# The leads of four layers re-ordered: rounding ahead, squares by pairs, two additions on GpSimd instead of four, angles during the first load

## The reference

```python
def rms_norm(x, g):
    xf = x.astype(jnp.float32)
    y = xf * lax.rsqrt(jnp.mean(xf * xf, axis=-1, keepdims=True) + RMS_EPS)
    return (y * g.astype(jnp.float32)).astype(x.dtype)

for l in range(DEPTH):                       # first block
    xn = rms_norm(h, norm_mix[l])
    proj = xn @ w_in[l]
    ...                                      # attention with top-k keys, short conv, RWKV-7 scan
    h = h + mixed @ w_out[l]
    h = h + conv_glu_ffn(rms_norm(h, norm_ffn[l]), ffn_up[l], ffn_conv[l], ffn_down[l])
h = rms_norm(h, norm_final)
for layer in range(DEPTH):                   # second block
    u = rms_norm_2(h, norm_w[layer], RMS_EPS) @ w_in[layer]
    ...                                      # dilated and differential attention, gates
    h = h + merged @ w_out[layer]
return rms_norm_2(h, final_norm_w, RMS_EPS)
```

## Time and profile before

| | before |
|---|---|
| median of 3 executions | 1776.34 us (1774.9 to 1778.92) |
| profiled execution, its own time | 1774.47 us |
| its span, first to last instruction | 1772.6 us |
| busy: PE, DVE, ACT, POOL | 96%, 64%, 52%, 11% of the span |
| chain that ended last | PE 75%, DVE 14%, ACT 6%, POOL 2% |
| mean granted TensorE clock | 0.98 of full speed |

### The profile page before, as it was taken

How to read it: one execution, slowest core, us unless ns; L and a number is a source line. 1 busy time by engine, 2 the same in 40 slices (tenths; PEclk the granted TensorE clock), 3 DMA queues, 4 the chain that set the end, 5 groups by cost and what they waited for, 6 DMA issues and landing times.

```text
span 1772.6 us, 30818 instructions
## 1 busy us (share of the span) xinstructions
PE 1708.3 (96%) x13020; PEld 1548.0 (87%) x13020; DVE 1138.3 (64%) x1601; ACT 930.3 (52%) x1369; POOL 195.2 (11%) x214
## 2 busy tenths in 40 slices
PE   6999999899998999999999999999999989999998
PEld 5988999899997988998899998888788878887887
DVE  6867455576666966446676666656766546567654
ACT  5473424454445583424454455665674446656742
POOL 1453400100001544300100000000000010000000
PEclk8999999899999999999899999999999989999998
DMA  5433433345544433432455545434345444343451
GB/s 206 172 135 99 151 128 120 135 174 185 176 167 159 165 120 102 156 121 95 167 186 179 191 165 190 145 141 166 119 146 196 158 167 152 133 166 119 158 195 51
DMA packets 48057, 268.34 MB, mean 151 GB/s; under 512 B 13552, under 2 KB 14448, under 8 KB 16176
## 3 DMA queue, kind: packets, MB, share of 16 engines
q1 hardware_dynamic: 38448, 264.80, 42.0%
q10 hardware_dynamic: 8704, 0.53, 0.3%
q0 software_dynamic: 768, 1.05, 0.2%
HBM read 264.52 MB, written 1.84 MB: 150 GB/s over the span
## 4 chain that ended last, share of the span: by engine, by line
PE 75%; DVE 14%; ACT 6%; POOL 2%; issue 2%; DMA 1%; SPq 0%; DVEq 0%; POOLq 0%; ACTq 0%
PE bank L1328 13%; PE bank L1329 13%; PE bank L1330 13%; PE bank L2413 8%; PE bank L2415 8%; PE bank L2414 8%; DVE w_low L866 4%; ACT arena L2046 1%; ACT arena L613 1%; ACT w_high L550 1%; PE bank L2484 1%; DVE small L2271 1%; PE bank L1555 1%; PE bank L2443 1%; DVE arena L2267 1%
## 5 line engine op out<-in xcount | busy, mean ns | idle before, releaser
L866 DVE TENSOR_TENSOR w_low<-slab,w_high 128x2048 fp32r<-128x2048 f32 x250 | 581.6, 2330 | 248.3 <-ACT w_high L550 247.4
L1328 PE MATMUL bank<-act_high,w_high 128*128 128x256 f32 x2304 | 663.6, 288 | 8.8 <-DVE act_low L932 4.9
L1329 PE MATMUL bank<-act_low,w_high 128*128 128x256 f32 x2304 | 655.5, 284 | 0.0
L1330 PE MATMUL bank<-act_high,w_low 128*128 128x256 f32 x2304 | 655.1, 284 | 0.0
L550 ACT ACTIVATE w_high<-slab 128x2048 fp32r<-128x2048 f32 x250 | 473.9, 1898 | 163.2 <-PE bank L2415 80.3
L1328 PEld LDWEIGHTS bank<-act_high,w_high 128*128 128x128 f32 x2304 | 445.6, 193 | 19.6 <-issue 11.9
L1329 PEld LDWEIGHTS bank<-act_low,w_high 128*128 128x128 f32 x2304 | 445.9, 194 | 0.6 <-issue 0.5
L1330 PEld LDWEIGHTS bank<-act_high,w_low 128*128 128x128 f32 x2304 | 445.7, 193 | 0.0
L2413 PE MATMUL bank<-w_high,act_high 128*128 128x512 f32 x768 | 306.5, 399 | 1.6 <-DVE w_low L866 1.6
L2415 PE MATMUL bank<-w_low,act_high 128*128 128x512 f32 x768 | 300.8, 392 | 0.0
L2414 PE MATMUL bank<-w_high,act_low 128*128 128x512 f32 x768 | 300.3, 391 | 0.0
(11 more groups left out here) (237 smaller groups left out, 1640.8 us busy)
## 6 DMA issues: line engine op xcount, KB each, us to landing
slab<-stream_a SPq DMA_DIRECT2D x144, 1024.0 KB, 4.8
slab<-stream_b SPq DMA_DIRECT2D x104, 1024.0 KB, 4.8
residual<-x_t SPq DMA_DIRECT2D x4, 256.0 KB, 5.9
lora_weights<-lora SPq DMA_DIRECT2D x2, 512.0 KB, 7.8
out_t<-residual SPq DMA_DIRECT2D x4, 256.0 KB, 2.1
d_inverse<-arena POOLq DMA_DIRECT2D x2, 256.0 KB, 3.3
constants<-common SPq DMA_DIRECT2D x1, 390.0 KB, 8.9
constants_a<-const_a SPq DMA_DIRECT2D x1, 368.0 KB, 8.9
```

The costliest lines, as they stand in the source:

```text
L866: line.did(line.eng.tensor_tensor(core.wl[u % PARTS][:, 0:SLAB_WIDTH[u]], core.slab[u % SLABS][:, 0:SLAB_WIDTH[u]], core.wh[u % PARTS][:, ...
L1328: eng.matmul(out, wh, xh, start=first, stop=False, skip_group_check=True)
L1329: eng.matmul(out, wh, xl, start=False, stop=False, skip_group_check=True)
L1330: return eng.matmul(out, wl, xh, start=False, stop=last, skip_group_check=True)
```

## The change

1. `lead_steps`, stages a1, b0, b1: the round of slab 1 is made at the end of the stage ahead, before its last unit, and ACT then loads the Sqrt table; both stood behind the four `scaled` steps. The squares of pairs 0 and 1 are made after their `scaled`, before `scaled` of pairs 2 and 3.
2. `pool_gather` in a0, a1, b1: two additions instead of four. Pair 1 is added to pair 0 and pair 3 to pair 2, each with its own signal, and TensorE sums four tiles (0, 1, 4, 5) with 8 one-column products instead of 2.
3. Stage a0: the angles are computed on DVE before the split of slab 0, and ACT takes their sines before the round of slab 1; the Sqrt table is loaded after that, and no longer after the mean. For this the 12 constants `inv` move to the table of gains, which is loaded early, and the load of the positions is issued third instead of eighth.
4. The small Sqrt that forces the table load stands ahead of the wait for the first square in the two ffn norms and at the end.

```diff
 def lead_steps(first):
+    halves = [[("scaled", 2 * n), ("scaled", 2 * n + 1)] for n in range(2)]
     if first:
-        return [("scaled", 0), ("scaled", 1)]
-    steps = []
-    for pair in (0, 2):
-        steps += [("add", pair), ("add", pair + 1), ("scaled", pair), ("scaled", pair + 1)]
-    return steps
+        return (halves[0] + [("angles", 0), ("round", 0), ("split", 0)] + halves[1] + [("angles", 1), ("round", 1), ("split", 1),
+                ("root_table", 0)] + [("square", i) for i in range(4)] + [("gather", 0), ("angles", 2)])
+    steps = [("root_table", 0)]
+    for n in range(2):
+        steps += [("add", 2 * n), ("add", 2 * n + 1)] + halves[n] + [("square", 2 * n), ("square", 2 * n + 1)]
+    return steps + [("gather", 0), ("split", 1)]
...
-    steps, rounded, n = list(lead), 0 if first else 1, len(units)
+    steps, rounded, n = list(lead), 2, len(units)
...
-    squares = [("square", i) for i in range(4)] + [("gather", 0)]
-    if first:
-        steps += ready(0) + [("scaled", 2), ("scaled", 3)] + ready(1) + squares
-    else:
-        steps += ready(1) + squares
     for u in range(n):
         ahead = u + PARTS - 1
-        split_next = ready(ahead) if ahead < n + (not last) else []
+        split_next = ready(ahead) if ahead < n + (not last) else [] if last else [("round", ahead)]
...
         if i == 0:
             eng.dma_start(core.gains[:], d["gains"]).then_inc(sem("gains_in").sem, 16)
+            eng.dma_start(core.turn[:, 192:194].bitcast(I32), d["positions"]).then_inc(sem("pos_in").sem, 16)
         if i == 1:
             slab_to(core, eng, 0)
     slab_to(core, eng, 1)
-    eng.dma_start(core.turn[:, 192:194].bitcast(I32), d["positions"]).then_inc(sem("pos_in").sem, 16)
...
         if i == 0:
-            square(0, True, True)
+            for at in (0, 1, 4, 5):
+                if at == 4:
+                    eng.wait_ge(*core.sem("gathered").next(eng))
+                square(at, at == 0, at == 5)
...
     for i in range(1, n):
         line.eng.wait_ge(*core.sem("squared").upto(first + i + 1))
-        line.settled()
-        line.did(line.eng.tensor_tensor(total, total, core.a(SQ_ + 2 * i, 2), ALU.add))
-    if n == 4:
-        line.settled()
-        line.did(line.eng.tensor_tensor(core.a(SQ_), core.a(SQ_), core.a(SQ_ + 1), ALU.add))
-    line.tell(core.sem("gathered"))
+        if n == 3 or i == 1:
+            line.settled()
+            line.did(line.eng.tensor_tensor(total, total, core.a(SQ_ + 2 * i, 2), ALU.add),
+                     core.sem("gathered") if (n, i) != (3, 1) else None)
+        elif i == 3:
+            line.did(line.eng.tensor_tensor(core.a(SQ_ + 4, 2), core.a(SQ_ + 4, 2), core.a(SQ_ + 6, 2), ALU.add),
+                     core.sem("gathered"))
```

More of the change, by code:

```diff
@@ L330 @@
 MORE = {"a0": dict(angles=1, angles_turned=1, dve_emptied3=-1, dve_emptied4=-1, dve_emptied5=-1, dve_emptied6=-1),
-        "b0": dict(diagonal=1, gathered=-1, norm_spread=1, rescaled=1, rooted_sums=1, second_mean=1)}
+        "b0": dict(diagonal=1, gathered=-2, norm_spread=1, rescaled=1, rooted_sums=1, second_mean=1)}
 START = stage_starts()
@@ L404, in amid @@
         mid.setdefault(unit, []).extend(steps)
-    if first:
-        put(("w", 0), ("angles", 0))
     amid(("w", 1), ("sum", 0), ("norm", 0), ("tables", 0))
@@ L563, in act_square, with act_root_table @@
 def act_square(core, line, i):
-    if i == 0:
-        line.did(line.eng.activation(core.small[:, ROOT_:ROOT_ + 1], core.small[:, 0:1], ACT.Sqrt))
     line.did(line.eng.activation(core.a(SQ_ + 2 * i, 2), core.h[:, 2 * i:2 * i + 2, :], ACT.Square), core.sem("squared"))
+def act_root_table(core, line):
+    line.did(line.eng.activation(core.small[:, ROOT_:ROOT_ + 1], core.small[:, 0:1], ACT.Sqrt))
 def act_root(core, line, sums):
@@ L622, in square @@
         if i >= 4:
+            if i == 4:
+                act_root_table(core, line)
             emptied(core, eng, rows, UA["out", i - 4])
@@ L640, in params, with angles @@
         eng.wait_ge(sem("vec_in").sem, 16 + 16 * layer)
-    def angles(_):
+    def angles(part):
+        if part != 1:
+            return
         eng.wait_ge(*sem("angles").next(eng))
@@ L831, in gn @@
                 act(core.xh[:, 2 * b:2 * b + 2, :], core.a(YC_ + 2 * b, 2), ACT.Copy, sem("yc_high"))
-    walk(SCHEDULE[stage], dict(params=params, angles=angles, round=act_round(core, line, FIRST_SLAB[stage]), scaled=scaled,
+    walk(SCHEDULE[stage], dict(params=params, root_table=lambda _: act_root_table(core, line), angles=angles, round=act_round(core, line, FIRST_SLAB[stage]), scaled=scaled,
                                square=square, norm=norm, norm_x=lambda _: high(8), unit=unit, turns=turns, isc=isc,
@@ L850, in scalar_program @@
     for i in range(4):
+        if i == 0:
+            act_root_table(core, line)
         residual(core, eng, "end", i)
@@ L918, in norm @@
     def norm(which):
+        if stage == "a0" and which == 0:
+            eng.wait_ge(sem("const_in").sem, 16)
         at = (SCALE_, RSTD_)[which]
@@ L1238, in gn @@
                 low(2 * b, 2, core.a(YC_ + 2 * b, 2), "yc_high", "yc_ready")
-    walk(SCHEDULE[stage], dict(params=params, angles=lambda _: rope_angles(core, line), add=dve_add(core, line),
+    walk(SCHEDULE[stage], dict(params=params, angles=lambda part: rope_angles(core, line, part), add=dve_add(core, line),
                                split=dve_split(core, line, FIRST_SLAB[stage]), scaled=scaled, norm=norm, tables=tables,
@@ L1252, in cu_tile, with rope_angles @@
     return core.ar[:, CU_ * T:CU_ * T + 4 * (T + 2)].rearrange("p (j t) -> p j t", j=4)
-def rope_angles(core, line):
+def rope_angles(core, line, part):
     eng, did, sem = line.eng, line.did, core.sem
     ts, stt = eng.tensor_scalar, eng.scalar_tensor_tensor
+    if part == 1:
+        return
+    if part == 2:
+        rope_tables(core, line)
+        return
     eng.wait_ge(sem("pos_in").sem, 16)
-    eng.wait_ge(sem("const_in").sem, 16)
     pos, n = flat(core, ANG_ + 2)[:, 0:2], flat(core, ANG_ + 2)[:, 8:32]
@@ L1270, in rope_angles @@
     for m in range(2):
-        did(ts(sin[:, 12 * m:12 * m + 12], core.const("inv", 12), pos[:, m:m + 1], None, ALU.mult))
+        did(ts(sin[:, 12 * m:12 * m + 12], core.gains[:, GN["inv"]:GN["inv"] + 12], pos[:, m:m + 1], None, ALU.mult))
     line.settled()
@@ L1288, in rope_angles, with rope_tables @@
     line.tell(sem("angles"))
-    eng.wait_ge(*sem("angles_turned").next(eng))
+def rope_tables(core, line):
+    eng, did, ts = line.eng, line.did, line.eng.tensor_scalar
+    eng.wait_ge(*core.sem("angles_turned").next(eng))
     turned = flat(core, ANG_ + 1)
@@ L2160, in merge @@
         act(core.xh[:, 8 + 2 * i:10 + 2 * i, :], heads(bank[7], T), ACT.Copy, sem("merged_high"))
-    walk(SCHEDULE[stage], dict(round=act_round(core, line, FIRST_SLAB[stage]), scaled=scaled, square=square, norm=norm, lam=lam, unit=unit,
+    walk(SCHEDULE[stage], dict(root_table=lambda _: act_root_table(core, line), round=act_round(core, line, FIRST_SLAB[stage]), scaled=scaled, square=square, norm=norm, lam=lam, unit=unit,
                        qk_turn=qk_turn, scores=scores, turn=turn, pv=pv, silu=silu, rms=rms, post=post, gate=gate,
@@ L2578, in constant_table @@
         b[:, CB["sin"] + 16 * m:][:, :16] = np.concatenate([np.sin(ang), -np.sin(ang)], 1)
-    return common, a, b
+    return common, a, b, np.broadcast_to(np.concatenate([inv64, inv32]), (P, 12))
 def tiles(w, starts):
@@ L2655 @@
     g = {k: np.asarray(v) for k, v in inputs.items()}
-    common, const_a, const_b = constant_table()
+    common, const_a, const_b, inv = constant_table()
     vec_a = np.concatenate(
@@ L2672 @@
          by_layer(columns(g["norm_w_2"])), g["final_norm_w_2"].reshape(KD, P).T, by_layer(columns(g["subln_w_2"])),
-         by_layer(lam), by_layer(lam_init)], 1)
+         by_layer(lam), by_layer(lam_init), inv], 1)
     arrays = {
```

9 lines of the change are left out of this document (4 added, 5 removed).

## The result

| | before | after |
|---|---|---|
| median, beside each other | 1777.3 us (4 executions) | 1757.46 us (1754.53 to 1763.67, 4 executions) |
| ratio | | 0.9894, 95% interval 0.9865 to 0.9924 |
| profiled execution, its own time / span | 1774.47 / 1772.6 us | 1754.53 / 1752.6 us |
| mean granted TensorE clock | 0.980 | 0.986 |
| same kernel once more (5 executions, beside 15 of before) | 1777.85 us | 1760.95 us, ratio 0.991, 0.9895 to 0.9924 |

The kernel became faster, by 16 to 19 us where 14.1 were forecast. The forecast as a ratio is 0.992, which lies inside both intervals, so the medians alone do not refute the sum; its parts are judged from the profiles.

A forecast was written before the change was run, and what follows sets the result against it. TensorE, busy 96% of the span, could win only idle and slow stretches, chiefly waits for GpSimd in a1 and b1. 5.4 + 8.4 + 0.4 - 0.1 = 14.1 us, so 1776.34 - 14.1 = 1762.2 us, range 1758.5 to 1767.

The forecast's parts named there:

- The long waits and their place: Leads of a1 and b1: TensorE's waits for GpSimd of 4.57 and 6.38 us before the sum of squares vanish.
- first rival: The forecast itself: both long waits in a1 and b1 vanish and the clock stays up; 1759 to 1765 us, chance 0.76.
- b1, 8.4 us: Lead of b1: first product of unit 2 at 1420.7 instead of 1428.97, 8.4 us less.
- a1, 5.4 us: Lead of a1: unit 1 and its sum end at 550.7 instead of 555.99, 5.4 us less.
- 1.7 for slow products: Lead of a1: the slow products behind the gap of 4.6 us go with it, 1.7 us of the gain.
- b0, 0.4: Lead of b0, which has no GpSimd part: only the earlier split counts, 0.4 us less.
- b0's 32 did not: Claim that a run of tiny products does not lower the clock, taken from the 32 two-column passes in b0.
- The end, 0: Ffn norms and the end: the moved small Sqrt gains a tenth of a microsecond or nothing, booked as 0.
- rival 2: In a1 and b1 GpSimd's addition starts before the split, which waits 1.3 us each; 1764.8 or 1766 us, chance 0.14.
- a0, "0.1 us more": Head of the program, stage a0: net 0.1 us more, bounds 0.5 less and 2.0 more.
- The gap less the passes: In a0 the dry 2.15 us before the spread vanish, less 1.4 for 12 more passes: 0.8 us won.
- positions ... I take 0.9: In a0 the earlier load of the positions delays the first product by 0.33 to 1.3 us, taken as 0.9.

The follow-up runs named there:

- leads: Kernel before with only the re-ordered leads of a1, b0, b1 and the moved small Sqrt, four additions kept: 1763.99 us, ratio 0.9925.
- head: Kernel before with only the new stage a0 (early angles and sines, positions loaded third): 1772.47 us, ratio 0.9968.
- no_head: Changed kernel without its new stage a0, that is re-ordered leads and two additions on the old start: 1758.72 us, ratio 0.9897.
- sums: Kernel before with only two additions instead of four and 8 one-column products: 1758.48 us, ratio 0.9888.

## Why the prediction was right and where it failed

- **The long waits and their place** (forecast, first rival): right. No wait for GpSimd in the leads; the asked-for times (2.9 us into unit 1, 16 passes of 0.115 us) came as reckoned.
- **b1, 8.4 us**: right, 8.56 and 8.49 in two profiles, and 9.4 alone (interval 7.3 to 11.7). The clock of 1.00 that it rested on stayed.
- **a1, 5.4 us**: the waits went as forecast, but 3.75 and 3.77 were measured at the stage's border. Up to the spread the gain was 11.7 - 6.2 = 5.5 us; 1.7 were given back behind it. The sum had booked 1.7 for slow products that would go with the gap ("the stretches behind have clock 1.00"); they did not go, as 546:570 has 0.86 before and after.
- **b0, 0.4**: 0.46 in one profile. In the other the clock fell to 0.66 there. "b0's 32 did not" pull the clock down was read from one execution and doesn't hold for each.
- **The end, 0**: 1.04 in both profiles, and no run explains it.
- **The addition in front of the split** (rival 2): not in the changed kernel, by 0.35 us; it came in *leads*, at a price of 1.1 us for each lead, 1.3 forecast.
- **a0, "0.1 us more": this step failed.** The profiles show 6.20 and 6.63 us less; *head* alone 5.7 (3.4 to 8.0). The gap less the passes was right: 1.0 us by the profile of after, 0.8 forecast. Three terms were not. First, "positions ... I take 0.9": SP issued it in 0.42 us in all seven profiles with the early load. As eighth issue it took 0.57 to 1.57 us in the seven others, so the 1.30 of the earlier trace rows did not belong to this DMA as such. The first product was no later for it: 12.50 to 13.15 us in the seven profiles with the early load, 12.22 to 14.12 in the seven with the late one, and 0.6 earlier in after than in before. Second, the slow products behind the dry spell: I counted them in a1 (1.7) and in b1 but not in a0, where before had a clock of 0.66 in 28:43. After won 3.3 us over these products. That the missing gap won them is not shown, since no_head and sums_head have no gap there and the same 0.66; this cause stays open. Third, 1.1 us come of the start, where products follow each other by 0.43 us at first and then by 0.23. That change comes 5.7 us after the first product in before and 3.1 in after, but 3.9 in *sums*, whose start is that of before, and 6.1 in *head*, whose start is that of after. So this part does not follow the change and is put down to chance.
- **The addition of parts.** The sum treated the leads as causes of one wait each. The runs show that part 1 and part 2 remove the same wait, and that part 2 frees the head as well. The forecast did not need this to be right, but a reader of the sum would have priced part 1 far too high.
- **The adding up.** The sum's own steps give 555.99 - 550.7 = 5.3 in a1 and 1428.97 - 1420.7 = 8.3 in b1; "with rounding" added 0.1 to each.

## What to carry to other kernels

Where an idle stretch of TensorE is removed, cost the slow products behind it in each place where it occurs, the program's head included, and read the clock of that stretch, in more than one execution, before writing zero or booking it as won. Before a chain is re-ordered, shorten what stands at its end: two additions fewer on GpSimd gave all that the new order gave, and freed VectorE elsewhere. The time of a DMA issue did not carry over from one place in SP's queue to another: 0.57 to 1.57 us as eighth issue, 0.42 as third. A profile is one execution: compare its time with the median before a stage is priced from it.

## What was not expected of the hardware

- The cast of 128x2 took 1.26 us in before and 0.15 in sums; a copy of 128x8 in after took 1.29 us while GpSimd's addition (18.29, 1.31 us) ran, and copies of that size beside no addition 0.16 or 0.17. Even these smallest VectorE operations, begun just after an addition, lasted until its end:

```profile
18.33 1.29 DVE L1311 COPY rotation<-arena 128x8 f32<-128x8 f32 x1
...
18.29 1.31 POOL L1993 TENSOR_TENSOR arena<-arena 128x512 f32<-128x512 f32 x1 [17.84 <-ACT arena L560]
```

- The granted clock fell in places where TensorE was never idle, in some executions and not in others: 1058:1068 at 1.00 and at 0.66 in two profiles of one kernel. That stage alone differs by 3.3 us between them, and their spans by 2.9.
